# Strassen's seven block products for gate and up, in two token sets, in a two-layer hybrid decoder trunk

## What is computed

```python
mix = jnp.concatenate([o_gla, o_lru, o_mla], axis=-1) @ w_out
x = _layer_norm(DEEPNORM_ALPHA * x + gate1 * mix, ln1_g, ln1_b)
h2 = x * (1 + scale2) + shift2
g_ff, u_ff = jnp.split(h2 @ ffn_w_gu, 2, axis=-1)        # D_FF = 2816
f = (jax.nn.silu(g_ff) * u_ff) @ ffn_w_down
x = _layer_norm(DEEPNORM_ALPHA * x + gate2 * f, ln2_g, ln2_b)
```

## Time and profile before

| | |
|---|---|
| three runs | 3607.07, 3608.55 and 3609.83 us, median 3608.55 |
| the profiled execution | 3609.93 us, its span 3608.1 us |
| mean granted clock of TensorE | 0.959 of full speed |
| TensorE busy | 3374.2 us, 94% of the span |
| VectorE / ScalarE / GpSimd busy | 41% / 32% / 5% |
| HBM read | 237.2 MB, 68 GB/s read and written over the span |

### The profile page before, as it was taken

One profiled execution on the slowest core, in us unless ns is written; L12 is line 12 of the kernel. 1 busy time (PEld: TensorE's weight loads), 2 busy tenths in 40 slices (PEclk: granted clock), 3 DMA queues, 4 the chain that ended last, 5 costly groups with the idle time before them and its releaser, 6 DMA issues. The chain is left out here.

```text
span 3608.1 us, 53525 instructions
## 1 busy us (share of the span) xinstructions
PE 3374.2 (94%) x22492; PEld 2909.7 (81%) x22492; DVE 1475.5 (41%) x2862; ACT 1144.4 (32%) x2189; POOL 193.7 (5%) x252
## 2 busy tenths in 40 slices
PE   6987898998999999999989868999989999999998
PEld 5864566666999999999979535666669999999997
DVE  5136565445442223232442366644445322232326
ACT  5235454444241121211231445534433311111121
POOL 0011211110000000000000121111100000000000
PEclk9997999998999999999989869989989999999999
DMA  5144002442011111111011510044410111111111
GB/s 210 32 142 155 26 1 106 164 164 83 13 36 42 48 46 49 42 47 45 26 52 30 194 29 1 1 154 163 152 48 18 42 39 51 43 46 43 46 47 68
DMA packets 91572, 247.16 MB, mean 69 GB/s; under 512 B 11419, under 2 KB 45501, under 8 KB 80454
## 3 DMA queue, kind: packets, MB, share of 16 engines
q1 hardware_dynamic: 79814, 159.85, 13.7%
q0 software_dynamic: 11520, 83.89, 6.5%
HBM read 237.20 MB, written 6.51 MB: 68 GB/s over the span
## 5 line engine op out<-in xcount | busy, mean ns | idle before, releaser
L454 PE MATMUL psum<-h_hi,w_ffn_hi 128*128 128x384 f32 (+1 forms) x2112 | 696.7, 330 | 0.4 <-DVE h_lo L2297 0.4
L456 PE MATMUL psum<-h_hi,w_ffn_lo 128*128 128x384 f32 (+1 forms) x2112 | 693.3, 328 | 0.0
L455 PE MATMUL psum<-h_lo,w_ffn_hi 128*128 128x384 f32 (+1 forms) x2112 | 683.5, 324 | 0.0
L454 PEld LDWEIGHTS psum<-h_hi,w_ffn_hi 128*128 128x128 f32 x2112 | 396.4, 188 | 1.6 <-issue 1.0
L455 PEld LDWEIGHTS psum<-h_lo,w_ffn_hi 128*128 128x128 f32 x2112 | 396.4, 188 | 0.0
L456 PEld LDWEIGHTS psum<-h_hi,w_ffn_lo 128*128 128x128 f32 x2112 | 395.6, 187 | 0.0
L454 PE MATMUL psum<-ffn_act_hi,w_ffn_hi 128*128 128x384 f32 (+1 forms) x906 | 295.9, 327 | 0.0
L456 PE MATMUL psum<-ffn_act_hi,w_ffn_lo 128*128 128x384 f32 (+1 forms) x906 | 295.7, 326 | 0.0
L455 PE MATMUL psum<-ffn_act_lo,w_ffn_hi 128*128 128x384 f32 (+1 forms) x906 | 295.4, 326 | 0.0
L440 DVE SCALAR_TENSOR_TENSOR xT<-psum,adaT,xT 128x384 f32<-128x384 f32 (+1 forms) x240 | 136.1, 572 | 383.6 <-PE psum L456 383.6
L2313 DVE TENSOR_TENSOR ffn_act<-silu_tmp,psum 128x384 f32<-128x384 f32 x132 | 70.2, 532 | 543.7 <-PE psum L456 543.7
(11 more groups left out here) (401 smaller groups left out, 5935.9 us busy)
## 6 DMA issues: line engine op xcount, KB each, us to landing
w_ffn<-in_w_gu SPq DMA_DIRECT2D x88, 512.0 KB, 3.3
w_ada_pair<-in_w_ada SPq DMA_DIRECT2D x40, 1024.0 KB, 5.1
w_ffn<-in_w_down SPq DMA_DIRECT2D x32, 384.0 KB, 3.1
w_ada_first<-in_w_ada SPq DMA_DIRECT2D x4, 2048.0 KB, 20.9
w_out<-in_w_out SPq DMA_DIRECT2D x16, 512.0 KB, 7.4
w_ffn<-in_w_down SPq DMA_DIRECT2D x22, 320.0 KB, 2.9
w_in_T<-in_w_in_T SPq DMA_DIRECT2D x12, 512.0 KB, 4.4
z<-in_x_prompt SPq DMA_DIRECT2D x8, 512.0 KB, 6.6
```

Source lines behind the costliest of these rows:

```text
L454: pe.matmul(o, wh, xh, start=first, stop=False)
L455: pe.matmul(o, wh, xl, start=False, stop=False)
L456: return pe.matmul(o, wl, xh, start=False, stop=last)
```

## The change

Gate and up are computed in two token sets: A, 512 tokens in halves of 256, and B, 576 tokens in halves of 288 (`HALVES`). The weights of a block f, gate and up by the two halves of the 1024 inputs, are the four blocks of one matrix; the four blocks of the other are the two halves of the inputs by the two halves of the set's tokens. Strassen's scheme in the form with seven products (Winograd's) replaces the eight block products: each product has four chunks k and one half of the tokens. For it:

- `h_sum` forms four sums of token blocks, and `form_rounded` and `form_rest` split the seven forms, once for each set: A beside the end of the output projection and at the start, B beside the last down part of A.
- For every pair (m: block f in set A, then again in set B, 44 a layer) the queue of the sync engine brings the weights in four quarters (`pair_in`, 256 KB each, two sets of slots), `w_sum` forms four weight sums on VectorE, and the seven forms are rounded (`w_rounded`, ScalarE, 512 columns each) and their remainders taken (`w_rest`, VectorE), four products ahead.
- The products go to banks 0 to 3 in turn. VectorE adds each to what came before (`u2`, `u3`, `c22`, `u5`, `c11`, `c21`, `c12` in `step`); ScalarE copies the first, and takes two Silus of a half each; VectorE multiplies twice (`UR`), ScalarE rounds and VectorE takes remainders, half by half.
- Down follows after 3 pairs, or 2 in the last two parts of a set (`FPART`; 16 parts `q` a layer): set A in 8 units of 512 columns, set B in 16 units of 288. The first two units of set A (four of set B) run without the last block first, and then wait for its remainder. Weights of down go through five slots.
- LN1 of the first four token blocks lies beside the output projection's second set, that of the other five beside pairs 0 and 1 of set A; LN2 of the first four beside pairs 25 and 26, in set B, of the next two beside the end of the last down part and after it, of the last three after that.
- The output projection runs in the same spans of 512, 288 and 288 columns.

The core of the diff. Left out are address layout, the norms' functions (they take their blocks in groups of 4, 2 and 3 and are called block by block), ScalarE's rounding calls and the output projection.

```diff
+        FPART = [(0, 3), (3, 6), (6, 9), (9, 12), (12, 15), (15, 18), (18, 20), (20, 22)]
+        PAIRS = [(pb * NF + f0, pb * NF + f1) for pb in range(2) for f0, f1 in FPART]
+        NQ = len(PAIRS)
+        PART = [q for q, (m0, m1) in enumerate(PAIRS) for _ in range(m0, m1)]
...
+        READY = [(1, 2, 5, 5, 6, 7, 7), (1, 2, 3, 4, 5, 6, 7)]
+        NU = [KD if q < NQ // 2 else 2 * KD for q in range(NQ)]
+        U0 = [sum(NU[:q]) for q in range(NQ + 1)]
+        NR, NW = 6, 5
...
+                    def pair_in(m):
+                        for slot, up_, k in ((0, 0, 0), (2, 1, 0), (4, 0, 4), (5, 1, 4)):
+                            if m >= 2:
+                                sp.wait_ge(s_pp, 7 * (m - 2) + slot + 1)
+                            src = a["w_gu"][bass.ds(layer[0], 1), 2 * (m % NF) + up_, :, k:k + 4]
+                            sp.dma_start(WGR[:, m % 2, slot], src.rearrange("o p k n -> (o p) k n")).then_inc(s_set[m % 2], 16)
...
+                    def products(m):
+                        pb = m // NF
+                        w = HALVES[pb][0][1]
+                        for i in range(7):
+                            j = 7 * m + i
+                            if m == 0 and i == 0:
+                                pe.wait_ge(s_ev, 3 * KD)
+                            if j >= 4:
+                                pe.wait_ge(bank_read[(j - 4) % 7], (j - 4) // 7 + 1)
+                            if m % NF == 0:
+                                pe.wait_ge(s_fl, 7 * pb + READY[pb][i])
+                            pe.wait_ge(s_wl, j + 1)
+                            xh, xl = form_hi(pb, i), form_lo(pb, i)
+                            for k in range(4):
+                                ins = three_passes(pe, bank(j % 4)[:, 0:w], WGH[:, (j + 1) % NR, k], WGL[:, m % 2, i, k],
+                                                   xh[:, k], xl[:, k], k == 0, k == 3)
+                            ins.then_inc(s_pp, 1)
+                            if m < 2:
+                                ln1_beside(j)
+                            if M2 <= m < M2 + 2:
+                                ln2_beside(j - 7 * M2)
...
+                    def down(q):
+                        m0, m1 = PAIRS[q]
+                        last, first = m1 - m0 - 1, 2 * NU[q] // KD if q < NQ - 1 else 4
...
+                        pe.wait_ge(s_ul, 2 * m1 - 2)
+                        for u in range(first):
+                            c = units[u][0]
+                            pe.wait_ge(s_dl, KD * q + (c if q < NQ - 1 else 0) + 1)
+                            bank_free(u)
+                            for f in range(last):
+                                part(u, f)
+                        pe.wait_ge(s_ul, 2 * m1)
+                        for u in range(first):
+                            part(u, last).then_inc(s_dn, 1)
+                        for u in range(first, len(units)):
+                            c = units[u][0]
+                            pe.wait_ge(s_dl, KD * q + (c if q < NQ - 1 else c // 4) + 1)
+                            bank_free(u)
+                            for f in range(last):
+                                part(u, f)
+                            part(u, last).then_inc(s_dn, 1)
...
+                        if i == 0:
+                            act.wait_ge(s_pp, j + 1)
+                            if m:
+                                act.wait_ge(s_um, 2 * m - 1)
+                            act.copy(P1T[:, 0:w], bank(j % 4)[:, 0:w]).then_inc(s_p1, 1)
+                            if m > m0:
+                                act_rounded(m - 1, 0)
+                                act_rounded(m - 1, 1)
+                        if i == 4:
+                            act.wait_ge(s_c11, m + 1)
+                            act.activation(P1T[:, 0:w], P1T[:, 0:w], ACT.Silu).then_inc(s_sa, 1)
+                        if j + 5 < 7 * NPAIR:
+                            w_rounded(j + 5)
+                        if m == m1 - 1 and q < NQ - 1 and i < NW:
...
+                        if i == 6:
+                            if m == m1 - 1:
+                                act_rounded(m, 0)
+                            act.wait_ge(s_c12, m + 1)
+                            act.activation(U2T[:, 0:w], U2T[:, 0:w], ACT.Silu).then_inc(s_sb, 1)
+                            if m == m1 - 1:
+                                act_rounded(m, 1)
...
+                    def w_sum(m, p):
+                        w = WGR[:, m % 2]
+                        if p == 1:
+                            dve.wait_ge(s_set[m % 2], 64 * (m // 2 + 1))
+                            ins = dve.tensor_tensor(w[:, 3], w[:, 2], w[:, 5], ALU.add)
+                        if p == 2:
+                            ins = dve.tensor_tensor(w[:, 2], w[:, 0], w[:, 2], ALU.subtract)
+                        if p == 3:
+                            dve.wait_ge(s_ws, 4 * m + 1)
+                            ins = dve.tensor_tensor(w[:, 1], w[:, 3], w[:, 0], ALU.subtract)
+                        if p == 4:
+                            dve.wait_ge(s_ws, 4 * m + 3)
+                            ins = dve.tensor_tensor(w[:, 6], w[:, 4], w[:, 1], ALU.subtract)
+                        ins.then_inc(s_ws, 1)
+
+                    def w_rest(j):
+                        m, i = divmod(j, 7)
+                        dve.wait_ge(s_wh, j + 1)
+                        dve.tensor_tensor(WGL[:, m % 2, i].bitcast(F32R), WGR[:, m % 2, i], WGH[:, (j + 1) % NR],
+                                          ALU.subtract).then_inc(s_wl, 1)
+
...
+                        u1, u2, u3, c22 = (v[:, 0:w] for v in (P1T, U2T, U3T, C22T))
+                        if i == 0 and m > m0:
+                            up_gated(m - 1)
+                        if i:
+                            dve.wait_ge(s_pp, j + 1)
+                        if i == 1:
+                            if m:
+                                dve.wait_ge(s_um, 2 * m)
+                            dve.wait_ge(s_p1, m + 1)
+                            dve.tensor_tensor(u2, p, u1, ALU.add).then_inc(s_u2, 1)
+                            if m > m0:
+                                act_rest(m - 1, 0)
+                                act_rest(m - 1, 1)
+                        if i == 2:
+                            dve.wait_ge(s_u2, m + 1)
+                            dve.tensor_tensor(u3, p, u2, ALU.add).then_inc(s_u3, 1)
+                        if i == 3:
+                            dve.wait_ge(s_u3, m + 1)
+                            dve.tensor_tensor(c22, p, u3, ALU.add).then_inc(s_c22, 1)
+                            dve.tensor_tensor(u2, p, u2, ALU.add).then_inc(s_u5, 1)
+                        if i == 4:
+                            dve.tensor_tensor(u1, p, u1, ALU.add).then_inc(s_c11, 1)
+                        if i == 5:
+                            dve.tensor_tensor(u3, p, u3, ALU.add).then_inc(s_c21, 1)
+                        if i == 6:
+                            dve.wait_ge(s_u5, m + 1)
+                            dve.tensor_tensor(u2, p, u2, ALU.add).then_inc(s_c12, 1)
+                        if i == 2 and m + 1 < NPAIR:
+                            w_sum(m + 1, 1)
+                            w_sum(m + 1, 2)
+                        if i == 3 and m + 1 < NPAIR:
+                            w_sum(m + 1, 3)
+                            w_sum(m + 1, 4)
+                        if j + 4 < 7 * NPAIR:
+                            w_rest(j + 4)
+                        if i == 5:
+                            dve.wait_ge(s_sa, m + 1)
+                            dve.wait_ge(s_c21, m + 1)
+                            if q and m == m0:
+                                dve.wait_ge(s_dn, U0[q])
+                            dve.tensor_tensor(UR[:, m - m0, 0:w], u1, u3, ALU.mult).then_inc(s_um, 1)
+                        if i == 6 and m == m1 - 1:
+                            act_rest(m, 0)
+                            dve.wait_ge(s_c22, m + 1)
+                            up_gated(m)
+                            act_rest(m, 1)
+                        if m == m1 - 1 and q < NQ - 1 and 1 <= i <= NW:
+                            down_rest(q, i - 1)
+                        if m == NPAIR - 1 and i in (4, 5):
+                            tail_rest(i - 4)
...
+                    def down(q):
...
+                        if q == NQ // 2 - 1:
+                            for p in range(3):
+                                h_sum(1, p)
+                        for u, (c, span, b) in enumerate(down_units(q)):
+                            dve.wait_ge(s_dn, U0[q] + u + 1)
+                            if q and q != NQ // 2:
+                                dve.wait_ge(s_dv, U0[q - 1] + (u + 1 if q < NQ - 1 else 2 * (u % KD) + 2))
+                            residual(dve, lk2, s_dv, TMPF, bank(b), c, span, M_G2)
+                            if q < NQ - 1 and c in (2, 3, 4) and (u + 1) % (NU[q] // KD) == 0:
```

(63 more changed lines are left out.)

857 lines of the change are left out of this document (520 added, 337 removed).

## The result

| | time, us | ratio to the kernel before | span, mean granted clock |
|---|---|---|---|
| before, four runs | 3607.94 (3607.07 to 3609.83) | 1 | 3608.1, 0.959 |
| changed, four runs | 3727.78 (3724.45 to 3734.02) | 1.0337, 95% interval 1.0321 to 1.0352 | 3732.2, 0.937 |

The account below looks back on a forecast made before the run. TensorE's matmul issue bounds the kernel before. Columns -130.7, boundary pauses +127.2, start +17, middle +15, LN2 +14, tail +9.5 and clock +24 sum to +76 us: 3684 us, range 3570 to 3770.

Parts of the forecast that it names:

- The lag of VectorE and the pauses: Part boundaries before down: TensorE stands while VectorE's late queue reaches the last activation remainder; +127.2 us over two layers.
- The clock: After pauses at the 32 part boundaries: half clock loses 0.75 us each, +24 us, ends 0 and 54.
- such a spell: Behind a pause: 3.4 us at 1.2 GHz, beginning 3.2 us after a 3.76 us pause began in the earlier trace.
- each boundary pays: Part boundaries: by the skill's rule, pauses between matmul bursts bring half clock, so every boundary loses time.
- The columns: Gate and up: seven products instead of eight stream 7/8 of the columns, -130.7 us over two layers.
- the rival's 0.145 us: Set A's products: a 256-column matmul costs what 320 columns do; 3726 us in all, chance 0.07.
- Start, middle, LN2: Start of products, change from set A to B, LN2 beside late pairs: other idle time +17, +15, +14, together +46 us.
- the start's 10.4 us: Before product 0: added wait for five blocks' LayerNorm in VectorE's queue (15.3 us), with 8.7 us of TensorE transposes beside it.
- The tail: Behind the last down matmul: the norm before the last has less matmul cover, 7 us for 17.5; +4 and +5.5, +9.5 us.
- Absorbed: Rival at part boundaries: VectorE's lag is absorbed, TensorE stays the bound, clock holds; 3533 us, 0.17 for ending faster.
- the sentence against it: Against the rival that VectorE's idle time absorbs the lag, the prediction set the order of VectorE's queue.
- Waits inside VectorE's steps: Rival in VectorE's steps: six more ops a pair pay the dependent price, +63 us, 3747 us in all, chance 0.14.

Follow-up runs that it names:

- late_weights: Changed kernel with VectorE's weight sums and remainders for the next part (and ScalarE's casts) moved from a part's last pair to between down's residuals: 3589.63 us, ratio 0.9955.
- four_units_first: Changed kernel with four down units of set A, not two, run without the last block before the wait: 3671.31 us, ratio 1.0175.
- clock_kept_A: Changed kernel with 18 extra matmuls of 512 columns, results unread, in TensorE's pause at each set A part boundary: 3702.85 us, ratio 1.0272.
- four_first_casts_first: late_and_four_first with ScalarE's casts of the sixth to eighth down weight put before the deferred gate and up casts: 3593.65 us, ratio 0.9956.
- late_and_four_first: Changed kernel with the edits of late_weights and four_units_first together: 3633.18 us, ratio 1.0073.

## Why the prediction was right or wrong

- **The lag of VectorE and the pauses: right, in place, cause and size.** Sixteen a layer, ended by ffn_act_lo. Set A 5.1 predicted at three-pair parts and 5.0 at two-pair ones, 4.56 and 4.79 measured; set B 3.0, 3.9 and 1.1, measured 2.86, 3.79 and 1.59. The parts that have a norm beside them are longer, 5.5 and 3.3 to 4.4. In sum 127.2 against 124.0 us. VectorE's prices held: 684 ns for 512 columns, 418 for 256. late_weights took the pauses away by order alone, and four_units_first shortened them by the cover it added.
- **The clock: the term that was mis-sized.** The prediction took "such a spell" as the 3.4 us of the earlier trace rows, of which 1.5 are left after a 5.1 us pause: 0.75 lost at each of 32 boundaries, +24, with 54 as the far end. The runs show twelve spells of 6.8 us and four of 3.4 behind set A's 16 pauses; the one shown begins 2.6 us into a 4.56 us pause, so 4.9 us of matmuls run in it and 2.5 are lost, and the sixteen lose 38 us. Ten of set B's 16 boundaries have a spell, 1.7 to 2.8 us lost, 23 us. Another 15 us are lost beside the norms, LN1 above all, where the kernel before lost 3 and the prediction priced no spell. Measured +74, beyond the stated end. clock_kept_A confirms set A's share, 37 us. The 50 us missing here are the whole miss: with the others (+16, -3, -17, +8 and -6 in the stages ahead) they make the 48 between forecast and profiled execution, 44 by the medians. That the others nearly cancel is luck. The rule of the Trainium skill that was weighed there (TensorE: Matmul & The Clock Gate, "Why this matters for your kernels") has long enough pauses between bursts bring half clock, not all of them, as "each boundary pays" took it: the trace agrees for pauses of 4.56 us, all of them, and shows it behind a part of the shorter ones (the last table here, down to 1.84 us).
- **The columns: mis-sized by 16 us.** 0.1165 and 0.131 us for a matmul of 256 and 288 columns were read off a line of three wider forms. Measured 0.1188 and 0.1329 on average. The timeline of the changed kernel, twelve matmuls of 256 columns apart:

```profile
1139.78 0.27 PE L422 MATMUL psum<-h_hi,w_ffn_hi 128*128 128x256 f32 x1
...
1141.20 0.28 PE L422 MATMUL psum<-h_hi,w_ffn_hi 128*128 128x256 f32 x1
```

  1.42 us for twelve. Over 7392 matmuls, two layers of 1848 of each width, 2.3 and 1.9 ns more make 16 us. So a narrow matmul costs some 2 ns more than the line of the wide ones, far less than the rival's 0.145 us.
- **Start, middle, LN2: too dear, +46 against +29.** The middle lost 4.0 us where 7.4 stood: four pauses of 1.74, 0.59, 0.60 and 0.70, and 0.41 more in set B's first part. How the start's 10.4 us come out of the 15.3 and 8.7 beside it, the prediction doesn't say.
- **The tail: too cheap, +9.5 against +17.6.** It is 8.5 us longer in the first layer and 9.1 in the last, where +4 and +5.5 stood. The one term that no experiment took apart, so its cause stays open.
- **The rivals.** "Absorbed" did not occur, and late_weights shows what kept it from occurring: the order of the queue, as the sentence against it said. Its time, 3533, is not reached by any version, since the norms, the start and the tail keep their part. Waits inside VectorE's steps cost nothing extra: without such a price the 32 pauses come to 127.2 us, measured 124.0. The 3747 of that rival is near the result for another reason, the clock.

## What to carry to other kernels

An engine with idle time can still stop the one that bounds: when it works ahead in program order, put what the next consumer waits for in front of what is needed later, on every queue of the chain, and count the tail at each boundary. A scheme that saves an eighth of the streamed columns of gate and up pays for its sums, splits and copies by that order: here the same work was 3.4% slower or 0.65% faster. And price a pause of TensorE with the clock behind it: here 124 us of pauses before down came with 61 us of half clock.

## What the runs showed of the hardware

The granted clock behind pauses before or within a down part, in the three-pair parts without a norm beside them, first layer, from the traces (the second layer has the same counts):

| pause, us | kernel, set | at 0.50 afterwards |
|---|---|---|
| 1.08 | four_first_casts_first, A | none of 5 |
| 1.84 | four_units_first, A | 1 of 5, for 3.4 us |
| 2.44 | late_and_four_first, A | 4 of 5, for 3.4 us |
| 2.86 | changed, B | 2 of 4, for 3.4 us |
| 4.56 | changed, A | 5 of 5: four for 6.8 us, one for 3.4 |

So the price of a pause isn't in proportion to its length: cutting 4.56 to 1.84 took 2.7 us of standing and about 2 of slow matmuls away. With five pauses or fewer to a row, the table gives a trend and no limit. And GpSimd, idle in this stage, was no help at all to a VectorE that reads two operands from SBUF: a weight remainder that overlapped one of its additions took 0.8 us longer, 1479 ns for 679.
